# A hybrid decoder trunk on one core: the order of the high and low weight products within a unit of TensorE work

## The chip, the core and the metric

The kernel runs on one NeuronCore of one Trainium2 chip. The metric is the device time of one execution in microseconds (us), as the median of several executions. TensorE multiplies matrices, VectorE (DVE in the rows), ScalarE (ACT) and GpSimd (POOL) compute elementwise, and SyncE (SP) starts the DMA transfers.

## What is computed

A trunk of two layers is run for one prompt of 512 tokens and for 8 samples of 4 new tokens, with the same weights, all in 32-bit floats. Each layer is a half feed-forward block (SwiGLU), a mixer, and another half feed-forward block. The mixer of layer 0 is a convolution module, that of layer 1 gated linear attention (GLA).

```python
def swiglu_ffn(h, w_gate, w_up, w_down):
    return (jax.nn.silu(h @ w_gate) * (h @ w_up)) @ w_down

for i in range(DEPTH):
    x = x + 0.5 * swiglu_ffn(rms_norm(x, norm_ffn_pre[i]), ffn_w_gate[i, 0], ffn_w_up[i, 0], ffn_w_down[i, 0])
    h = rms_norm(x, norm_mix[i])
...
    x = x + y
    x = x + 0.5 * swiglu_ffn(rms_norm(x, norm_ffn_post[i]), ffn_w_gate[i, 1], ffn_w_up[i, 1], ffn_w_down[i, 1])
```

In the lines left out y is the mixer's result. The convolution module is a projection from 1024 to 2048 (`pw1`), a gate, a depthwise convolution of 31 taps, a layer norm and a projection (`pw2`). GLA projects to queries, keys, values, an output gate and a decay (`gz`, `gv`, `gr`, `gkq`), runs a recurrence over matrix states, and projects back (`gwo`). The model width is 1024 (8 blocks of 128), the feed-forward width 2816 (22 blocks). Outputs are the final normed activations and the new convolution and GLA states.

## The kernel before

The 544 tokens (512 and 32) stand along the free dimension, features along the 128 partitions. Every activation tensor is a row of blocks of 128 x 544.

**Three products for one.** A weight product in full precision is made of three products of a reduced 32-bit type. The weight `raw` is split into `w_hi` (a copy into the reduced type, by ScalarE, `high`) and `w_lo` (`raw - w_hi`, by VectorE, `low`); the activations likewise into `xg_hi` and `xg_lo`, or `h_hi` and `h_lo`. TensorE adds `w_hi * a_hi`, `w_hi * a_lo` and `w_lo * a_hi` in PSUM. Each product of a block is two matmuls, since 544 columns are two halves of 272 in two banks. Every matmul loads its 128 x 128 weights anew.

**Slots.** Weights come in slots of up to 8 blocks of 128 x 128, 512 KB each, numbered through the whole program (329 of them). SyncE loads a slot into one of 2 `raw` places, and waits before that for `w_split` of the slot that used the place. `w_hi` and `w_lo` are rings of 4 places. ScalarE writes `w_hi` of slot n after `w_done` of slot n - 4 and counts `w_high` up; VectorE waits for `w_high`, writes `w_lo` and counts `w_split` up. TensorE counts `w_done` up with the last matmul of a slot. Each engine's instructions stand in a fixed order, written out by hand, and semaphores join the engines.

**Units.** A unit is one output block of 128 x 544, in one of four pairs of PSUM banks. An up projection or a square one takes one slot for a unit (48 matmuls), a down projection three slots, of 8, 8 and 6 blocks (132 matmuls). VectorE takes the result out of PSUM and counts `evac` up; TensorE waits on `evac` before it writes over a pair.

**`slot_products`** makes the products of one slot. It waits for `w_split` of its slot, and then goes through the blocks k: for each of them six matmuls, `w_hi` with `a_hi`, `w_hi` with `a_lo`, `w_lo` with `a_hi`, two halves each. With `ready` it waits ahead of each block until the activation of that block is split: `x_split` for the first slot of the convolution's first projection (`pw1`) and for `gz`, the first slot of the GLA stage; `h_split` for the first unit of each down projection. With `halfway` a function is called ahead of the block in the middle: in the GLA output projection (`gwo`) it is `sample_kv(i)`, four matmuls for the samples' states `st`, which VectorE then updates (line 1903). **`wide_products`** (line 480 on) does the first two or four slots of the other stages at once and is a function of its own; the last unit of the program has its own code (line 1336).

**What follows the two slots that wait for `x_split`.** Behind the first slot of `pw1`, and behind `gz`, stands `pe_stat` (line 518): two matmuls that sum the squares of x, after `acc` of GpSimd (line 627). VectorE and ScalarE make the reciprocal root of it (lines 642 to 651, 661, 663), with which all evictions of that stage are scaled. `xg_hi` (line 602, ScalarE) and `xg_lo` (line 608, VectorE) of block m are made after x of block m has been updated with the result of the down projection (line 808, VectorE).

Of the kernel before, what the change touches and what calls it, by code (L numbers as in the profile page):

```python
# [42 lines left out]
def build(nc, x_prompt, x_sample, state_conv, state_gla, norm_ffn_pre, norm_mix, norm_ffn_post, norm_final,  # L43
# [7 lines left out]
    HALF = T // 2  # L51
# [18 lines left out]
    with ctx:  # L70
# [7 lines left out]
        def sb(name, shape, dt=F32):  # L78
            n = 4
            for d in shape[1:]:  # L80
                n *= d
            offset = taken[0]
            taken[0] += (n + 31) // 32 * 32
            return at(name, shape, dt, offset)
# [10 lines left out]
        w_hi = sb("w_hi", [P, RING, SLOT_K, P], F32R)  # L95
        w_lo = sb("w_lo", [P, RING, SLOT_K, P], F32R)
# [109 lines left out]
        ps = nc.alloc_psum_tensor("ps", [P, 8, 512], F32)  # L206
# [8 lines left out]
        def sem(name):  # L215
            return ctx.enter_context(nc.semaphore(name))
# [14 lines left out]
        w_high = sem("w_high")  # L231
        w_split = sem("w_split")
# [232 lines left out]

        def slot_products(pe, n, pair, a_hi, a_lo, nk=SLOT_K, k0=0, kt=SLOT_K, i=0, per=0, ready=None, halfway=None):

            pe.wait_ge(w_split, n + 1 + per * i)
            r = n % RING
            for k in range(nk):  # L470
                if ready is not None:
                    pe.wait_ge(ready[0], ready[1] + k + 1)
                if halfway is not None and k == nk // 2:
                    halfway()
                for w, a in ((w_hi, a_hi), (w_hi, a_lo), (w_lo, a_hi)):
                    for c in range(2):
                        last = nc.tensor.matmul(  # L477
                            ps[:, 2 * pair + c, 0:HALF], w[:, r, k, :], a[:, k0 + k, c * HALF:(c + 1) * HALF],
                            start=(k0 + k == 0 and w is w_hi and a is a_hi),
                            stop=(k0 + k == kt - 1 and w is w_lo))  # L480
            last.then_inc(w_done, 1)

        def wide_products(pe, n, pairs, a_hi, a_lo, ready, high_ready=None, between=None):
# [56 lines left out]
        def pe_ffn(pe, s):  # L540
            u0, s0 = s.up.u0, s.up.s0
            if s is f00:
                pe.wait_ge(evac, 2)
                pe.wait_ge(s_xo, 2)
                wide_products(pe, s0, [u0 % 4, (u0 + 1) % 4], xg_hi, xg_lo, (x_split, 0))

                pe.wait_ge(s_diag, TT + 1)
                bank = 2 * ((u0 + 3) % 4)
                for t in range(TT):
                    nc.tensor.matmul(ps[:, bank, t * P:(t + 1) * P], ones[:, :], rdiag[:, t, :], start=True, stop=True)  # L550
                nc.tensor.matmul(ps[:, bank + 1, 0:NS], ones[:, :], rdiag[:, TT, 0:NS], start=True, stop=True).then_inc(
                    s_stat, 1)
                slot_products(pe, s0 + 2, (u0 + 2) % 4, xg_hi, xg_lo)
                pe.wait_ge(s_r0, 1)
                slot_products(pe, s0 + 3, (u0 + 3) % 4, xg_hi, xg_lo)
            else:
                pe.wait_ge(evac, u0 - 2)
                wide_products(pe, s0, [u0 % 4, (u0 + 1) % 4], xg_hi, xg_lo, (x_split, M * s.q))
                pe.wait_ge(evac, u0)
                pe_stat(pe, s.e, (u0 + 3) % 4)  # L560
                slot_products(pe, s0 + 2, (u0 + 2) % 4, xg_hi, xg_lo)
                pe.wait_ge(s_nv, 3 * s.r + 1)
                slot_products(pe, s0 + 3, (u0 + 3) % 4, xg_hi, xg_lo)
# [1439 lines left out]
```

## Time and profile before

| | |
|---|---|
| median of 3 runs | 2128.21 us (2127.31 to 2129.12) |
| the profiled execution | 2128.8 us |
| its span, first to last instruction | 2127.1 us |
| TensorE matmul busy | 2086.6 us, 98% |
| VectorE busy | 990.8 us, 47% |
| ScalarE busy | 637.7 us, 30% |
| GpSimd busy | 142.7 us, 7% |
| DMA, mean share of 16 engines | about 31% |
| matmuls on line 477 | 3 x (3344 + 1524) |

All rows come from one profiled execution. Matmuls are pipelined: each row shows some 0.29 us for one, but they start closer together, so I read their pace from start to start. A share of busy time is a mean over stages; what an edit is worth has to be read at the place where it acts.

### The profile page before, as it was taken

Reading aid. Unit: us, or ns where it says so; the run is one execution under the profiler, and the core shown is the slowest. Engines: PE = TensorE matmul, PEld = TensorE weight load, DVE = VectorE, ACT = ScalarE, POOL = GpSimd, SP = SyncE. Lnnn points to the kernel's source line nnn. Section 1 sums busy time; section 2 is a strip of 40 time slices with the busy share of each in tenths; the row PEclk is TensorE's granted clock in tenths of the full one; section 3 lists DMA queues with packets and bytes.
Section 4 is the critical chain, followed back from the end, with each engine's and each line's share of the span. In section 5 each row is a group of like instructions: output and inputs, shape, how many; then the busy total and the mean of one; then the engine's idle time right before and its main releaser. Section 6 shows DMA issues by size and latency. Waiting matters only on the chain.

```text
span 2127.1 us, 39290 instructions
## 1 busy us (share of the span) xinstructions
PE 2086.6 (98%) x16373; PEld 2026.5 (95%) x16373; DVE 990.8 (47%) x1299; ACT 637.7 (30%) x899; POOL 142.7 (7%) x146
## 2 busy tenths in 40 slices
PE   8999999999899999999999999999999999999998
PEld 7999999987599999999999999999888899999998
DVE  4575433387655444433344443333455764444332
ACT  5222222222243222222322222222433532222222
POOL 2000001200021000011100000111000210000000
PEclk9999999999999999999999999999999999999999
DMA  5232323345323223232333332232224333332322
GB/s 165 80 92 85 89 82 92 94 119 141 85 60 99 82 86 88 87 90 82 88 90 89 89 89 82 84 91 82 73 61 130 104 116 89 89 88 83 95 83 70
DMA packets 351727, 194.83 MB, mean 92 GB/s; under 512 B 8636, under 2 KB 345758, under 8 KB 351628
## 3 DMA queue, kind: packets, MB, share of 16 engines
q1 hardware_dynamic: 345388, 185.10, 30.3%
q10 hardware_dynamic: 4560, 4.82, 0.7%
q0 software_dynamic: 1696, 3.73, 0.6%
q8 instruction: 62, 1.02, 0.2%
q14 instruction: 21, 0.17, 0.0%
HBM read 177.29 MB, written 8.05 MB: 87 GB/s over the span
## 4 chain that ended last, share of the span: by engine, by line
PE 92%; DVE 3%; ACT 2%; issue 1%; DMA 1%; SPq 1%; POOL 0%; DVEq 0%; ACTq 0%
PE ps L477 83%; PE ps L488 3%; PE ps L1067 1%; PE ps L1336 1%; ACT w_hi L455 1%; PE ps L1076 1%; SPq L886 0%; DMA raw<-in_ffn_w_gate 0%; DVE cv L1660 0%; DVE odd_sum L1660 0%; DMA raw<-in_conv_w_pw 0%; PE ps L1183 0%; DVE x L1721 0%; PE ps L1191 0%; DMA st<-in_state_gla 0%
## 5 line engine op out<-in xcount | busy, mean ns | idle before, releaser
L477 PE MATMUL ps<-xg_hi,w_hi 128*128 128x272 f32 x3344 | 696.8, 290 | 4.0 <-DVE tb L1677 2.0
L477 PE MATMUL ps<-xg_hi,w_lo 128*128 128x272 f32 x3344 | 693.8, 289 | 0.0
L477 PE MATMUL ps<-xg_lo,w_hi 128*128 128x272 f32 x3344 | 691.0, 288 | 0.0
L455 ACT ACTIVATE w_hi<-raw 128x1024 fp32r<-128x1024 f32 x329 | 348.2, 1059 | 1025.8 <-PE ps L477 977.7
L462 DVE TENSOR_TENSOR w_lo<-raw,w_hi 128x1024 fp32r<-128x1024 f32 x329 | 412.7, 1255 | 411.8 <-ACT w_hi L455 411.4
L477 PEld LDWEIGHTS ps<-xg_hi,w_hi 128*128 128x128 f32 x3344 | 527.4, 189 | 7.4 <-DVE tb L1677 3.1
L477 PEld LDWEIGHTS ps<-xg_lo,w_hi 128*128 128x128 f32 x3344 | 526.7, 189 | 0.0
L477 PEld LDWEIGHTS ps<-xg_hi,w_lo 128*128 128x128 f32 x3344 | 523.2, 189 | 0.0
L477 PE MATMUL ps<-h_hi,w_hi 128*128 128x272 f32 x1524 | 316.0, 289 | 1.4 <-DVE x L1721 0.9
L477 PE MATMUL ps<-h_hi,w_lo 128*128 128x272 f32 x1524 | 315.8, 289 | 0.0
L477 PE MATMUL ps<-h_lo,w_hi 128*128 128x272 f32 x1524 | 314.4, 288 | 0.0
L477 PEld LDWEIGHTS ps<-h_hi,w_hi 128*128 128x128 f32 x1524 | 239.6, 188 | 1.9 <-DVE x L1721 1.1
L477 PEld LDWEIGHTS ps<-h_lo,w_hi 128*128 128x128 f32 x1524 | 239.6, 189 | 0.0
L477 PEld LDWEIGHTS ps<-h_hi,w_lo 128*128 128x128 f32 x1524 | 237.9, 189 | 0.0
L778 DVE TENSOR_TENSOR tb<-ps,rB 128x544 f32<-128x544 f32 x88 | 63.7, 724 | 284.3 <-PE ps L477 284.3
L701 ACT ACTIVATE h_hi<-tb 128x544 f32 (+1 forms) x88 | 58.0, 659 | 178.1 <-DVE tb L783 178.1
L774 DVE TENSOR_TENSOR ta<-ps,rB 128x544 f32<-128x544 f32 x88 | 63.7, 724 | 98.4 <-PE ps L477 97.5
L785 DVE TENSOR_TENSOR h_lo<-tb,h_hi 128x544 f32 (+1 forms) x88 | 63.9, 726 | 82.6 <-ACT h_hi L701 82.6
L627 POOL TENSOR_TENSOR acc<-acc,sqt 128x544 f32<-128x544 f32 x35 | 64.7, 1849 | 2.8
L620 POOL TENSOR_TENSOR acc<-x 128x544 f32<-128x544 f32 x5 | 5.5, 1092 | 873.6 <-DVE x L808 817.9
L783 DVE TENSOR_TENSOR tb<-ta,tb 128x544 f32<-128x544 f32 x88 | 63.2, 719 | 0.0
L698 ACT ACTIVATE ta<-ta 128x544 f32<-128x544 f32 x88 | 56.8, 645 | 20.0 <-DVE ta L774 20.0
(273 smaller groups left out, 1213.2 us busy)
## 6 DMA issues: line engine op xcount, KB each, us to landing
raw<-in_ffn_w_gate SPq DMA_DIRECT2D x88, 512.0 KB, 3.8
raw<-in_ffn_w_up SPq DMA_DIRECT2D x88, 512.0 KB, 3.8
raw<-in_ffn_w_down SPq DMA_DIRECT2D x64, 512.0 KB, 4.0
raw<-in_gla_w_in SPq DMA_DIRECT2D x25, 512.0 KB, 3.8
raw<-in_ffn_w_down SPq DMA_DIRECT2D x32, 384.0 KB, 3.4
raw<-in_conv_w_pw SPq DMA_DIRECT2D x24, 512.0 KB, 4.4
u_shift<-uext SPq DMA_DIRECT2D x112, 66.0 KB, 2.0
raw<-in_gla_w_out SPq DMA_DIRECT2D x8, 512.0 KB, 4.2
```

Of the source, the lines that this page charges most:

```text
L455: nc.scalar.activation(w_hi[:, n % RING], raw[:, n % RAW], ACT.Copy).then_inc(w_high, 1)
L462: nc.vector.tensor_tensor(w_lo[:, n % RING], raw[:, n % RAW], w_hi[:, n % RING].bitcast(F32), ALU.subtract).then_inc(w_split, 1)
L477: last = nc.tensor.matmul(ps[:, 2 * pair + c, 0:HALF], w[:, r, k, :], a[:, k0 + k, c * HALF:(c + 1) * HALF], start=(k0 + k == 0 and w is w ...
L488: last = nc.tensor.matmul(ps[:, 2 * pairs[j] + c, 0:HALF], w[:, (n + j) % RING, k, :], a[:, k, c * HALF:(c + 1) * HALF], start=(k == 0 and ...
L627: last = nc.gpsimd.tensor_tensor(acc[:, :], acc[:, :], sqt[:, :], ALU.add)
L698: nc.scalar.activation(ta[:, p, :], ta[:, p, :], ACT.Silu).then_inc(a_done, 1)
L701: nc.scalar.activation(h_hi[:, 2 * i + p, :], tb[:, p, :], ACT.Copy).then_inc(h_high, 1)
L774: nc.vector.tensor_tensor(halves(ta[:, p, :]), bank_pair(pair), halves(rB[:, :]), ALU.mult).then_inc(evac, 1)
L778: nc.vector.tensor_tensor(halves(tb[:, p, :]), bank_pair((pair + 1) % 4), halves(rB[:, :]), ALU.mult).then_inc(evac, 1)
L783: nc.vector.tensor_tensor(tb[:, p, :], ta[:, p, :], tb[:, p, :], ALU.mult).then_inc(h_prod, 1)
L785: nc.vector.tensor_tensor(h_lo[:, 2 * i + p, :], tb[:, p, :], h_hi[:, 2 * i + p, :].bitcast(F32), ALU.subtract).then_inc(h_split, 1)
L1067: last = nc.tensor.matmul(ps[g * GROUP:(g + 1) * GROUP, 4 + m % 2, :], w_tap[:, m % 2, g, n, :], u_shift[m % 3][:, g, SHIFTS * n:SHIFTS * ...
```

## The change

Within `slot_products` the products with `w_hi` now run over all blocks of the slot first, and those with `w_lo` over all blocks afterwards. The wait for `w_split` at the head of the slot becomes a wait for `w_high`, and the wait for `w_split` stands between the two passes. The waits of `ready` and the call of `halfway` stay in the first pass. `w_done` is counted up by the last matmul of the second pass.

```diff
-            pe.wait_ge(w_split, n + 1 + per * i)
+            def products(k, w, a):
+                for c in range(2):
+                    last = nc.tensor.matmul(
+                        ps[:, 2 * pair + c, 0:HALF], w[:, r, k, :], a[:, k0 + k, c * HALF:(c + 1) * HALF],
+                        start=(k0 + k == 0 and w is w_hi and a is a_hi),
+                        stop=(k0 + k == kt - 1 and w is w_lo))
+                return last
+
+            pe.wait_ge(w_high, n + 1 + per * i)
             r = n % RING
             for k in range(nk):
                 if ready is not None:
                     pe.wait_ge(ready[0], ready[1] + k + 1)
                 if halfway is not None and k == nk // 2:
                     halfway()
-                for w, a in ((w_hi, a_hi), (w_hi, a_lo), (w_lo, a_hi)):
-                    for c in range(2):
-                        last = nc.tensor.matmul(
-                            ps[:, 2 * pair + c, 0:HALF], w[:, r, k, :], a[:, k0 + k, c * HALF:(c + 1) * HALF],
-                            start=(k0 + k == 0 and w is w_hi and a is a_hi),
-                            stop=(k0 + k == kt - 1 and w is w_lo))
+                products(k, w_hi, a_hi)
+                products(k, w_hi, a_lo)
+            pe.wait_ge(w_split, n + 1 + per * i)
+            for k in range(nk):
+                last = products(k, w_lo, a_hi)
             last.then_inc(w_done, 1)
```

The end of the first slot of `pw1` on TensorE, before; each row is a line, an instruction and what it waits for, and `acc` is the sum of squares:

```order
L477 MATMUL ps<-xg_hi,w_hi 128x272 [waits x_split]
L477 MATMUL ps<-xg_hi,w_hi 128x272
L477 MATMUL ps<-xg_lo,w_hi 128x272 x2
L477 MATMUL ps<-xg_hi,w_lo 128x272 x2
L518 MATMUL ps<-acc,ones 128x272 [waits s_acc]
L518 MATMUL ps<-acc,ones 128x272
L477 MATMUL ps<-xg_hi,w_hi 128x272 [waits w_split,evac]
```

And with the change (line numbers are 7 higher behind the helper, and its matmul is on line 470):

```order
L470 MATMUL ps<-xg_hi,w_hi 128x272 [waits x_split]
L470 MATMUL ps<-xg_hi,w_hi 128x272
L470 MATMUL ps<-xg_lo,w_hi 128x272 x2
L470 MATMUL ps<-xg_hi,w_lo 128x272 [waits w_split]
L470 MATMUL ps<-xg_hi,w_lo 128x272 x15
L525 MATMUL ps<-acc,ones 128x272 [waits s_acc]
L525 MATMUL ps<-acc,ones 128x272
L470 MATMUL ps<-xg_hi,w_hi 128x272 [waits w_high,evac]
```

The last wait for `x_split` stood ahead of the last 6 matmuls of the slot; now it stands ahead of the last 20, of which 16 take `w_lo`. `gz` is built in the same way.

The middle of the first slot of `gwo` that has a `halfway`, on TensorE, before; `kem` and `v_s` are the operands of `sample_kv`:

```order
L477 MATMUL ps<-h_lo,w_hi 128x272 x2
L477 MATMUL ps<-h_hi,w_lo 128x272 x2
L1282 MATMUL ps<-v_s,kem 128x256 [waits g_kem,g_vlo]
L1282 MATMUL ps<-v_s,kem 128x256 x3
L477 MATMUL ps<-h_hi,w_hi 128x272 x2
L477 MATMUL ps<-h_lo,w_hi 128x272 x2
L477 MATMUL ps<-h_hi,w_lo 128x272 x2
```

And with the change:

```order
L1289 MATMUL ps<-v_s,kem 128x256 [waits g_kem,g_vlo]
L1289 MATMUL ps<-v_s,kem 128x256 x3
L470 MATMUL ps<-h_hi,w_hi 128x272 x2
L470 MATMUL ps<-h_lo,w_hi 128x272 x2
L470 MATMUL ps<-h_hi,w_hi 128x272 x2
L470 MATMUL ps<-h_lo,w_hi 128x272 x2
L470 MATMUL ps<-h_hi,w_hi 128x272 x2
L470 MATMUL ps<-h_lo,w_hi 128x272 x2
L470 MATMUL ps<-h_hi,w_hi 128x272 x2
L470 MATMUL ps<-h_lo,w_hi 128x272 x2
L470 MATMUL ps<-h_hi,w_lo 128x272 [waits w_split]
L470 MATMUL ps<-h_hi,w_lo 128x272 x15
```

Ahead of `sample_kv` there were 24 matmuls of the slot and 24 behind it; now there are 16 ahead and 32 behind.

## Rows read from the trace of the kernel before

**Rows 1.** The page's busy time (share of the span) and instructions of each engine.
```profile
PE 2086.6 (98%) x16373; PEld 2026.5 (95%) x16373; DVE 990.8 (47%) x1299; ACT 637.7 (30%) x899; POOL 142.7 (7%) x146
```
**Rows 2.** The chain that ended last: start us, us, what, how many.
```profile
52.86 366.85 PE ps L477 x2928
...
1034.53 12.06 PE ps L488 x96
```
**Rows 3.** Waits: engine, line, waited for: us in total, times, longest us.
```profile
ACT w_hi L455 <- PE ps L477: 977.7, 279, 5.9
...
PE ps L1076 <- DVE cv L1670: 5.4, 1, 5.4
```
**Rows 4.** Timeline of `pw2`: start us, us, engine, line, operation, count, idle before.
```profile
609.59 1.23 DVE L462 TENSOR_TENSOR w_lo<-raw,w_hi 128x1024 fp32r<-128x1024 f32 x1 [12.12 <-ACT w_hi L455]
...
611.56 0.52 PE L477 MATMUL ps<-h_hi,w_hi 128*128 128x272 f32 x2 [0.85 <-DVE x L1721]
```
**Rows 5.** Stretches: us, busy us (count) by engine, PEclk, DMA share, GB/s.
```profile
660.00:780.00 120.00, 120.00 (x960) 120.00 (x959) 54.66 (x63) 34.89 (x42) 0.00 (x0) 1.00 0.32 92
820.00:1030.00 210.00, 210.00 (x1679) 210.00 (x1678) 76.66 (x81) 52.56 (x58) 18.57 (x13) 1.00 0.30 88
```
**Rows 6.** Timeline of the first slot of `pw1`.
```profile
419.53 0.41 PE L477 MATMUL ps<-xg_hi,w_hi 128*128 128x272 f32 x2
...
423.84 0.79 DVE L608 SCALAR_TENSOR_TENSOR xg_lo<-x,par,xg_hi  x1 [1.16 <-ACT xg_hi L602]
423.93 1.90 POOL L627 TENSOR_TENSOR acc<-acc,sqt 128x544 f32<-128x544 f32 x1
...
424.78 0.42 PE L477 MATMUL ps<-xg_hi,w_hi 128*128 128x272 f32 x2
...
425.88 1.19 PE L518 MATMUL ps<-acc,ones 128*128 128x272 f32 x4 [0.19 <-POOL acc L627]
```
**Rows 7.** Timeline of TensorE where it starts again in `pw1`.
```profile
463.83 0.52 PE L477 MATMUL ps<-xg_hi,w_hi 128*128 128x272 f32 x2 [1.25 <-DVE tb L1677]
464.19 0.29 PE L477 MATMUL ps<-xg_lo,w_hi 128*128 128x272 f32 x1
```
**Rows 8.** Timeline of `gz`.
```profile
1432.18 0.41 PE L477 MATMUL ps<-xg_hi,w_hi 128*128 128x272 f32 x2
...
1436.49 0.79 DVE L608 SCALAR_TENSOR_TENSOR xg_lo<-x,par,xg_hi  x1 [1.16 <-ACT xg_hi L602]
...
1438.64 1.16 PE L518 MATMUL ps<-acc,ones 128*128 128x272 f32 x4 [0.28 <-POOL acc L627]
```
**Rows 9.** Timeline of the start of the first down projection.
```profile
291.33 0.73 DVE L785 TENSOR_TENSOR h_lo<-tb,h_hi 128x544 f32 x1 [0.94 <-ACT h_hi L701]
...
299.26 0.41 PE L477 MATMUL ps<-h_hi,w_hi 128*128 128x272 f32 x2
```
**Rows 10.** Timeline of the end of `gwo`, VectorE and TensorE.
```profile
1700.33 0.63 PE L1282 MATMUL ps<-v_s,kem 128*128 128x256 f32 x4
...
1701.17 1.65 DVE L1903 SCALAR_TENSOR_TENSOR st<-st,dec,ps 128x256 f32<-128x256 f32 x4
1702.74 2.21 DVE L462 TENSOR_TENSOR w_lo<-raw,w_hi 128x1024 fp32r<-128x1024 f32 x1
1704.87 1.64 DVE L1903 SCALAR_TENSOR_TENSOR st<-st,dec,ps 128x256 f32<-128x256 f32 x4
...
1715.20 0.49 PE L488 MATMUL ps<-xg_hi,w_hi 128*128 128x272 f32 x2 [1.75 <-issue]
```
**Rows 11.** Stretches, columns as in rows 5; the last of line 477 alone.
```profile
460.00:468.00 8.00, 6.75 (x60) 4.69 (x50) 7.78 (x12) 3.97 (x5) 0.00 (x0) 1.00 0.58 152
561.50:564.90 3.40, 3.16 (x10) 2.35 (x11) 0.79 (x2) 0.00 (x0) 0.00 (x0) 0.51 0.91 245
...
1496.80:1507.00 10.20, 9.49 (x33) 7.99 (x33) 3.63 (x5) 6.74 (x6) 0.00 (x0) 0.50 0.11 30
...
1501.60:1507.00 5.40, 5.40 (x24) 5.40 (x25) 0.50 0.00 2
```

## The prediction

> **What bounds the kernel now.** I read the busy shares first, then the chain that ended last, then who waits for whom, and after that the timeline at the places where TensorE pauses. TensorE computes for 2086.6 us of a span of 2127.1 us [rows 1], and 83% of the chain that ended last is one line, the matmul of `slot_products`. In the middle of a feed-forward stage 2928 of these matmuls follow each other in 366.85 us [rows 2], which is 0.1253 us each; I call this the pace. A slot of 8 blocks has 48 matmuls and so takes 6.01 us. A change of order pays only where TensorE now waits for something that it could do without a little longer, and it costs where TensorE now just finds ready something that it will want earlier.
>
> The change drops the wait for `w_lo` at the head of a slot. Does anybody wait there today? In the list of waits the longest that ends on a matmul is 5.4 us, for a tensor of the convolution, and neither `w_lo` nor `w_hi` stands anywhere in it as the releaser of a matmul. It is the other way round: ScalarE waited 279 times, 977.7 us in all, for TensorE to give a place of the ring back before it could write `w_hi` [rows 3]. The weights run ahead. I looked for the slot where they run ahead least, and it is the fifth of the second projection of the convolution: its `w_lo` ends at 609.59 + 1.23 = 610.82 us, but TensorE starts that slot at 611.56 us, released by the eviction of a result [rows 4]. So the wait that is dropped ends last nowhere, and I put the gain at 0.
>
> **The change part by part.** *The same matmuls.* No matmul is added or removed. A slot has 32 products with `w_hi` and then 16 with `w_lo`. What a matmul costs in the new order the trace of before does not show. The nearest rows are those of `wide_products`, which has a third order (high, low, high in each block): 96 matmuls in 12.06 us [rows 2], 0.1256 us each, 0.0003 us above the pace, and those include some ten waits. The new order changes between `w_hi` blocks and `w_lo` blocks no more often than the old one, so I take 0. For the range I keep 0.0003 us either way; line 477 has 3 x (3344 + 1524) = 14,604 matmuls, which is 4.4 us up or down.
>
> *The added wait.* Each of the 312 slots that go through this helper (329, less 14 of `wide_products` and the 3 of the last unit) gets one more wait, in its middle. What an already fulfilled wait costs can be read by comparing stretches: in the up projection every 48 matmuls have two waits and a branch of the loop falls on every 192; in the down projection four waits fall on 132 matmuls. Both run at 960 matmuls in 120 us and 1679 in 210 us [rows 5], 0.125 us each to the last digit that these counts allow. I take 0 and leave the cost of up to 0.003 us per wait that the ten waits of [rows 2] would give (1 us in all) inside the 4.4 us above.
>
> *The wait for `x_split`, block by block: the term that counts.* Two slots read their activations while these are still being made: the first of `pw1`, at 419.53 us, and `gz`, at 1432.18 us. They wait for `xg_lo` of block k ahead of block k. The last block, k = 7, is late, because `x` of that block can only be updated when the last down projection is done: its `xg_lo` runs from 423.84 to 424.63 us [rows 6]. Before, block 7 is reached after 7 x 6 = 42 matmuls, at 419.53 + 42 x 0.1253 = 424.79 us, and the row of that matmul says 424.78 us: it just meets the data, 0.15 us behind. Now the high part reaches block 7 after 7 x 4 = 28 matmuls, at 419.53 + 3.51 = 423.04 us. TensorE must stand until 424.63 + 0.06 = 424.69 us (0.05 us lie between the end of `acc` at 423.93 + 1.90 = 425.83 us and the matmul that it releases at 425.88 us; I take 0.06), that is 1.65 us. After a stop the first pair takes 0.36 us in place of 0.25 us [rows 7], another 0.11 us. Left of the slot are 4 matmuls of the high part and 16 of the low part: 20 x 0.1253 = 2.51 us, so it has issued its last at 424.69 + 0.11 + 2.51 = 427.31 us.
>
> Not all of this reaches the end. Right behind the slot stands the matmul of the sum of squares (line 518), which waits for that `acc` of GpSimd and starts at 425.88 us, while the slot's own matmuls ended at 425.54 us. Now `acc` has been ready for long and the matmul starts at 427.31 us: **+1.43 us**. What is late next is everything: VectorE's reciprocal root, the evictions of the first two units, and the copies that SyncE issues for the convolution all hang on that matmul or on the end of this slot, so the whole stage moves by as much and I see nothing in it that takes it back.
>
> The same for `gz` [rows 8]: block 7 is wanted at 1432.18 + 3.51 = 1435.69 us, `xg_lo` ends at 1436.49 + 0.79 = 1437.28 us, TensorE goes on at 1437.34 us, and issues its last at 1437.34 + 0.11 + 2.51 = 1439.96 us. The sum of squares started at 1438.64 us before: **+1.32 us**.
>
> The Trainium skill has a rule on this, in "TensorE: Matmul & The Clock Gate", under "What happens when you issue a matmul": the engine may pull a weight load forward, but matmuls stay in program order. By it the 16 products with `w_lo` cannot pass the blocked block 7; were they free to, the stop would be filled and the sum would be 0.
>
> *The slots that wait for `h_split`* (the first three of each down projection) are not near it: in the first of these stages the last `h_lo` ends at 291.33 + 0.73 = 292.06 us, and the third slot, the one that reads it, starts at 299.26 us [rows 9]. *The slots cut in half by `sample_kv`*: its four matmuls stood after 24 matmuls of the slot and now stand after 16, 1.0 us earlier. VectorE's updates of `st` behind them stand in a fixed order with other work: the last group runs from 1704.87 us because `w_lo` ahead of it takes from 1702.74 to 1704.95 us [rows 10], not because of its matmuls, so nothing comes earlier. The last of them waits for an update that ends at 1701.17 + 1.65 = 1702.82 us and is now wanted at 1700.33 + 0.47 + 16 x 0.1253 = 1702.80 us: up to 0.2 us of stop, and it lies ahead of a pause of 1.75 us that ends at 1715.20 us [rows 10] and that no matmul of this helper sets. I count 0.
>
> **Sum**: 1.43 + 1.32 = 2.75 us. The profiled execution took 2128.8 us (a span of 2127.1 us and 1.7 us around it), 0.6 us over the median of 2128.21 us. So 2131.5 us against itself, and 2131.0 us as a median. That is 0.13%. A measurement of this kernel tells about 0.2%, 4.3 us, from no change, and this would be called the same.
>
> **The rivals.** *Nothing is lost* (2128.2 us): while block 7 is missing TensorE would go on with the 16 products of `w_lo`, 2.00 us of work, which fills a stop of 1.65 us. Against it: in the order of before, too, work that was ready stood behind waiting matmuls, as the whole slot behind the 5.4 us of [rows 3], and none of it went ahead.
>
> *Slower, by the clock.* The granted clock fell twice in the middle of the kernel, both times after TensorE had been idle: at 561.5 us, to 0.51 for 3.4 us, and at 1496.8 us, to 0.50 (1.2 GHz) until 1507.0 us [rows 11]. In the second fall 24 matmuls took 5.40 us, 0.225 us each. If each new stop let the clock fall as at 561.5 us, that would be 3.4 x (1 - 0.1253/0.225) = 1.5 us each and 3.0 us in all: 2134.0 us. It decides once a stop of 1.65 us in a dense stretch is enough for the clock to fall. Against it: ahead of 463.83 us TensorE was idle for 1.25 us [rows 7], and the clock stayed at 1.00 [rows 11].
>
> *Slower, by the pace or the waits*: at the upper bound of 4.4 us, 2131.0 + 4.4 = 2135.4 us. The same bound downwards gives 2126.6 us.
>
> *Slower, by issue.* If a weight load and a matmul took half the pace each merely to be issued, TensorE would be bound by its instruction stream, and each of the 312 added waits would cost 0.0626 us: 19.5 us, 2150.5 us. Against it: at that price two waits per 48 matmuls and four per 132 would differ by 0.0007 us a matmul and the loop's branches by more, and [rows 5] show one pace. The Trainium skill, in the same page under "Wait — 56ns, not 53.3ns?", says that with hardware decode off the sequencer spends about 62 ns on each matmul, which would be just this case.
>
> **How the numbers follow.** The two stops: 0.68. Nothing lost: 0.10. Clock: 0.06. Pace or waits upwards: 0.10; downwards: 0.04. Issue: 0.02. The predicted time is 2131.0 us. The runs of before spread by 0.9 us about their median. The range from 2127.8 to 2134.2 us takes in the two stops with the spread and a part of the bound of the pace, nothing lost, and the clock. Faster by over 0.2% (under 2124.0 us) takes the whole downward bound and no stops: 0.03. Slower (over 2132.5 us) is clock, pace upwards, issue, and a tail of 0.04 of the first case: 0.22. The same: 0.75.
>
> **What would show it.** In the timeline after: at about 424.7 and 1438.7 us (moved by the first stop) a `xg_hi,w_hi` matmul with some 1.5 us of idle time ahead, released by `xg_lo`; in the list of waits the pair matmul and `xg_lo` with two waits and about 3 us. The sum-of-squares matmul at 427.3 us, and at 1438.64 + 1.43 + 1.32 = 1441.4 us. The loops at 366.9 us per 2928 matmuls; another pace there is the rival of the pace. A granted clock below 1.00 at 425 or 1438 us is the rival of the clock. I am wrong in the large if order alone changes what a matmul costs.

## The result, and the profile after

The change takes **2135.89 us** (median of 7 runs, 2135.77 to 2137.71), the kernel before, run beside it, 2128.21 us (7 runs, 2126.60 to 2131.52). The ratio is 1.0036, with a 95% interval of 1.0025 to 1.0048: slower by 7.7 us. The forecast was 2131.0 us with a range up to 2134.2 us. The change came out 4.9 us above the forecast and 1.7 us above the range; the two stops on which the forecast rests are 2.75 us. One execution of e3_waits_only below took 8598.58 us and one of e4_third_order 6119.55 us, for a reason that no row shows, and their ratios leave these out.

The profiled execution after took 2135.8 us, with a span of 2134.1 us, 7.0 us more than before. Its busy time by engine, as in [rows 1]: TensorE is busy 7.5 us longer, with the same number of matmuls (its weight loads, PEld, 6.5 us longer); the other engines stay within 0.9 us.

```profile
PE 2094.1 (98%) x16373; PEld 2033.0 (95%) x16373; DVE 990.9 (46%) x1299; ACT 638.2 (30%) x899; POOL 143.6 (7%) x146
```

**The stops are there, and as long as forecast.** The timeline of TensorE after, in the first slot of `pw1` and in `gz` (start us, us, engine, line, operation, count, idle before and its releaser), which answers to [rows 6] and [rows 8]:

```profile
420.41 0.41 PE L470 MATMUL ps<-xg_hi,w_hi 128*128 128x272 f32 x2
...
423.68 0.41 PE L470 MATMUL ps<-xg_lo,w_hi 128*128 128x272 f32 x2
425.56 0.52 PE L470 MATMUL ps<-xg_hi,w_hi 128*128 128x272 f32 x2 [1.47 <-DVE xg_lo L615]
...
426.16 2.18 PE L470 MATMUL ps<-xg_hi,w_lo 128*128 128x272 f32 x16
428.18 1.08 PE L525 MATMUL ps<-acc,ones 128*128 128x272 f32 x4
...
1436.54 0.41 PE L470 MATMUL ps<-xg_hi,w_hi 128*128 128x272 f32 x2
...
1441.69 0.52 PE L470 MATMUL ps<-xg_hi,w_hi 128*128 128x272 f32 x2 [1.46 <-DVE xg_lo L615]
...
1444.31 1.08 PE L525 MATMUL ps<-acc,ones 128*128 128x272 f32 x4
```

TensorE issues 28 matmuls of the high part and stops until `xg_lo` of block 7 is there. The 16 matmuls with `w_lo`, whose data is ready, stand behind. From the first matmul of the slot to the sum of squares it was 425.88 - 419.53 = 6.35 us in `pw1` and is 428.18 - 420.41 = 7.77 us now: +1.42 us, against a forecast of +1.43. In `gz` it was 1438.64 - 1432.18 = 6.46 us and is 1444.31 - 1436.54 = 7.77 us: +1.31 us, against +1.32. The list of waits (engine, line, waited for: total us, times, longest) has the new pair:

```profile
PE ps L470 <- DVE xg_lo L615: 2.9, 2, 1.5
...
PE ps L470 <- ACT w_hi L455: 1.2, 1, 1.2
```

The second row is new in name only. Before, the same place (1553.56 us, now 1560.34 us) waited 1.17 us, put down to VectorE's `ta`; now it waits 1.17 us, put down to the `w_hi` for which the change has TensorE wait. The ScalarE wait of [rows 3] hardly moved, 980.5 us.

The clock stayed at 1.00 across both stops (stretches: us, busy us and count of PE, PEld, DVE, ACT, POOL, PEclk, DMA share, GB/s), also from 424.05 to 425.56 us and from 1440.20 to 1441.70 us, the stops themselves:

```profile
425.00:427.00 2.00, 1.44 (x11) 1.45 (x12) 0.50 (x1) 0.85 (x1) 2.00 (x2) 1.00 0.60 180
1441.00:1443.00 2.00, 1.31 (x10) 1.31 (x11) 0.64 (x1) 0.98 (x1) 2.00 (x2) 1.00 0.75 218
```

**The loops are slower, and that was not forecast.** The chain that ended last (start us, us, what, how many), after:

```profile
51.79 368.80 PE ps L470 x2928
...
652.34 385.70 PE ps L470 x3072
1038.04 12.05 PE ps L495 x96
1051.01 385.71 PE ps L470 x3072
...
1734.64 275.72 PE ps L470 x2196
```

The same four runs of matmuls in the kernel before; its 366.85 us for 2928 stand in [rows 2]:

```profile
649.68 384.85 PE ps L477 x3072
...
1047.50 384.86 PE ps L477 x3072
...
1728.41 275.11 PE ps L477 x2196
```

TensorE waits for nothing in these runs. The pace was 0.1253 us in all four (384.85 / 3072 = 0.12528). It is 368.80 / 2928 = 0.12596 us in the first stage and 385.70 / 3072 = 0.12556 us in the other three. `wide_products` (line 495), which the change does not touch, needs 12.05 us for 96, and 12.06 us before.

The two traces, place by place; each row but the last is the start of the same matmul, and the last column is what was added since the row above:

| place | before | after | after is later by | grown by |
|---|---|---|---|---|
| first loop begins | 52.86 | 51.79 | -1.07 | |
| first slot of `pw1` | 419.53 | 420.41 | 0.88 | 1.95 |
| sum of squares of `pw1` | 425.88 | 428.18 | 2.30 | 1.42, stop |
| second loop | 649.68 | 652.34 | 2.66 | 0.36 |
| third loop | 1047.50 | 1051.01 | 3.51 | 0.85 |
| first slot of `gz` | 1432.18 | 1436.54 | 4.36 | 0.85 |
| sum of squares of `gz` | 1438.64 | 1444.31 | 5.67 | 1.31, stop |
| fourth loop | 1728.41 | 1734.64 | 6.23 | 0.56 |
| end of the span | 2127.1 | 2134.1 | 7.0 | 0.77 |

The loads at the start happened to be 1.07 us quicker in the execution after. From there it lost 8.07 us: 2.73 us in the two stops and 5.34 us elsewhere. Of these, 4.26 us lie in the four loops (1.95, 0.85, 0.85 and 0.61 us), 11,268 of the 14,604 matmuls of `slot_products`. The last 1.08 us are a sum of gains and losses. The largest is a stretch of low clock in GLA, here in 18 us of each trace, before and then after:

```profile
1490.00:1508.00 18.00, 14.98 (x68) 12.36 (x67) 6.63 (x7) 11.89 (x13) 1.03 (x2) 0.72 0.18 50
```
```profile
1494.00:1512.00 18.00, 15.69 (x66) 12.28 (x65) 5.09 (x6) 9.57 (x12) 1.03 (x2) 0.67 0.26 73
```

The granted clock was near 0.50 (1.2 GHz) until 1507.0 us before and until about 1513.9 us after, and from the slots behind `gz` to the run of 384 matmuls behind them it took 62.81 us in place of 61.77 us. The experiments e1 to e4 below need 61.75 to 61.85 us for the same way, with either order, and e7, the change with one more matmul at the start, needs 62.81 us again. So the order alone does not bring this 1 us; what does is open. The loops are the larger part, and the experiments are about them.

### The profile page after: what moved, and what is told of

Its sections match the earlier page's. It is cut to its first block, busy times and chain, and to the rows that moved or that the text cites. A ratio compares the mean times of both kernels' runs of the same rounds, so it can differ in the third digit from the quotient of the medians.

```text
span 2134.1 us, 39290 instructions
## 1 busy us (share of the span) xinstructions
PE 2094.1 (98%) x16373; PEld 2033.0 (95%) x16373; DVE 990.9 (46%) x1299; ACT 638.2 (30%) x899; POOL 143.6 (7%) x146
## 4 chain that ended last, share of the span: by engine, by line
PE 93%; DVE 2%; ACT 1%; DMA 1%; issue 1%; SPq 1%; DVEq 0%; ACTq 0%
PE ps L470 85%; PE ps L495 3%; PE ps L1074 1%; PE ps L1343 1%; PE ps L1083 1%; SPq L893 0%; ACT w_hi L455 0%; DVE cv L1667 0%; PE ps L1164 0%; DMA pin<-in_gla_onorm_g 0%; DVE odd_sum L1667 0%; PE ps L1190 0%; PE ps L1198 0%; DMA st<-in_state_gla 0%; DMA raw<-in_conv_w_pw 0%
## 5 line engine op out<-in xcount | busy, mean ns | idle before, releaser
L455 ACT ACTIVATE w_hi<-raw 128x1024 fp32r<-128x1024 f32 x329 | 348.5, 1060 | 1028.9 <-PE ps L470 980.5
L470 PE MATMUL ps<-xg_hi,w_lo 128*128 128x272 f32 x3344 | 452.9, 288 | 0.0
L470 PEld LDWEIGHTS ps<-xg_hi,w_lo 128*128 128x128 f32 x3344 | 432.2, 188 | 0.0
L470 PE MATMUL ps<-h_hi,w_lo 128*128 128x272 f32 x1524 | 207.7, 288 | 0.0
L470 PEld LDWEIGHTS ps<-h_hi,w_lo 128*128 128x128 f32 x1524 | 197.5, 188 | 0.0
L631 POOL TENSOR_TENSOR sqt<-x 128x544 f32<-128x544 f32 x35 | 40.1, 1145 | 331.1 <-DVE x L815 290.2
```

The costliest lines, as they stand in the source:

```text
L455: nc.scalar.activation(w_hi[:, n % RING], raw[:, n % RAW], ACT.Copy).then_inc(w_high, 1)
L470: last = nc.tensor.matmul(ps[:, 2 * pair + c, 0:HALF], w[:, r, k, :], a[:, k0 + k, c * HALF:(c + 1) * HALF], start=(k0 + k == 0 and w is w ...
L631: nc.gpsimd.tensor_tensor(sqt[:, :], src[:, m, :], src[:, m, :], ALU.mult).then_inc(p_acc, 1)
```

## Experiments

"This" and "before" are medians from the same chip; a ratio has its 95% interval. The edits are shown against the change, those of e12 and e13 against the kernel before.

### Which part of the change costs what

**e1_no_stop** is the change, but the two slots that wait for `x_split` keep the order of before.

```diff
+            together = ready is not None and ready[0] is x_split
...
+                if together:
+                    last = products(k, w_lo, a_hi)
```

> The change, but the two slots that wait block by block for the split activations (first slot of pw1, and gz) keep the order of before. Theory (stops and pace are two separate costs): the two stops of 1.75 us in the timeline at 425.56 and 1441.69 us go, the loops keep the pace of the changed kernel (368.8 us for 2928 matmuls in the first stage, 385.7 us for 3072 in the later ones), and the median falls by 2.7 us, from 2135.9 to 2133.2. Rival (the stops are all that matters and the pace is an accident of that execution): the median comes down to about 2128 to 2129.

**e2_order_only** has the new order with one wait for `w_split` at the head, as before.

```diff
-            pe.wait_ge(w_high, n + 1 + per * i)
+            pe.wait_ge(w_split, n + 1 + per * i)
...
-            pe.wait_ge(w_split, n + 1 + per * i)
```

> The new order of products, but one wait for w_split at the head of the slot as before, none in the middle. Theory A (the order itself costs the pace, some 0.0003 us a matmul): the loops stay at 385.7 us for 3072 matmuls and the median at 2135 to 2137. Rival B (the wait in the middle of the slot costs some 0.014 us each, 48 x 0.0003): the loops return to 384.9 us, only the stops are left, and the median is about 2131.

**e3_waits_only** has the old order with the two waits of the change.

```diff
-            pe.wait_ge(w_split, n + 1 + per * i)
-            for k in range(nk):
+                if k == 0:
+                    pe.wait_ge(w_split, n + 1 + per * i)
                 last = products(k, w_lo, a_hi)
```

> The order of products of before, but the two waits of the change: w_high at the head of the slot, w_split ahead of the first product with w_lo, after four matmuls. Theory A (order costs): loops at 366.9 us for 2928 and 384.9 us for 3072 matmuls, median 2128 to 2129. Rival B (the added wait costs): loops at 368 us or more and 385.7 us, median 2132 to 2134.

**e4_third_order** puts the order of `wide_products` (high, low, high in each block) into `slot_products`.

```diff
-            pe.wait_ge(w_high, n + 1 + per * i)
+            pe.wait_ge(w_split, n + 1 + per * i)
...
                 products(k, w_hi, a_hi)
-                products(k, w_hi, a_lo)
-            pe.wait_ge(w_split, n + 1 + per * i)
-            for k in range(nk):
-                last = products(k, w_lo, a_hi)
+                products(k, w_lo, a_hi)
+                last = products(k, w_hi, a_lo)
```

> One wait at the head, and in every block high with a_hi, low with a_hi, high with a_lo: the order of the helper that takes several slots at once, whose 96 matmuls took 12.06 us before (0.1256 us each). No stop, since the data of a block are wanted when before. Theory A (the order sets the pace, and this one has the pace of those 96): loops of 3072 matmuls at 385.8 us, median about 2133. Rival B (the 0.1256 us there come from that helper's ten waits): loops at 384.9 us, median 2128 to 2129.

| kernel | this, us | ratio to before (2127.75 us) | first loop, 2928 | third loop, 3072 |
|---|---|---|---|---|
| e1_no_stop | 2132.45 | 1.0021 (1.0012 to 1.0030) | 368.80 | 385.71 |
| e2_order_only | 2136.06 | 1.0039 (1.0026 to 1.0052) | 368.80 | 385.71 |
| e3_waits_only | 2127.13 | 0.9995 (0.9986 to 1.0005) | 366.84 | 384.86 |
| e4_third_order | 2127.51 | 0.9997 (0.9988 to 1.0006) | 366.84 | 384.86 |

The first loop in the chains of e2, then e3, then e4, from which the table is read:

```profile
51.68 368.80 PE ps L470 x2928
```
```profile
52.24 366.84 PE ps L470 x2928
```
```profile
52.81 366.84 PE ps L470 x2928
```

The order alone is the whole effect (e2), and the waits alone are nothing (e3). Without the stops the change is still slower by 0.21%, 4.7 us between the medians, with exactly the loops of the change (e1); the stops are the 3.6 us between e1 and e2, where the trace of the change has 2.73 us of them; the 0.9 us between are not explained. (Its two idle times are 1.47 and 1.46 us; the 1.75 us of the expectation are in no row.) And e4 takes away the row on which I sized the term: `wide_products` runs at 0.1256 us a matmul, yet with the order of its blocks `slot_products` runs at 0.1253. What sets `wide_products` apart is then something else. It has some ten waits in 96 matmuls, which would be 3 ns for each, while the 312 waits added in e3 cost nothing that shows; and it goes through two slots side by side, with other weights and other banks in turn, which e4 does not do. Neither was tried by itself.

### Does the rule lie in how often the weights change between high and low?

**e5_three_passes** makes three passes over the slot: high with `a_hi`, high with `a_lo`, low with `a_hi` (the `x_split` slots as in e1).

```diff
-                products(k, w_hi, a_lo)
...
+                for k in range(nk):
+                    products(k, w_hi, a_lo)
+                pe.wait_ge(w_split, n + 1 + per * i)
+                for k in range(nk):
+                    last = products(k, w_lo, a_hi)
```

> Three passes over the blocks of a slot instead of two: high with a_hi, then high with a_lo, then low with a_hi; the two slots that wait for the split activations keep the order of before, so there is no stop. Theory C (in the later stages of the changed kernel the pass with w_lo, which reads one activation tensor alone, runs at 0.1250 us a matmul and the pass with w_hi, which changes between a_hi and a_lo, at 0.1258; a pass on one tensor is the fast one): loops at 384.0 us for 3072 matmuls, median 2124 to 2126. Rival D (long passes are slow whatever they read): loops at 385.7 us or more, median 2132 or more.

It took 2125.85 us against 2127.59 us, a ratio of 0.9992 (0.9983 to 1.0001): the same. Its executions lie between 2123.64 and 2129.62 us, those of before between 2125.76 and 2128.99 us, and the profiled one is the slowest. Its chain is what counts:

```profile
51.81 368.46 PE ps L470 x2928
...
650.16 386.56 PE ps L470 x3072
...
1049.70 384.01 PE ps L470 x3072
```

The second and the third loop are the same instructions, and one runs at 0.1258 us, the other at 0.1250; the fourth, 274.50 us for 2196, is at 0.1250 too. So each of my two expectations came true in two loops of the four. One order has two paces, on either side of the pace of before, and holds each through a whole loop. Where pauses of 0.5 us stand between groups of 132 matmuls, in the last down projection, the groups take 16.51 and 16.61 us by turns, which are the same two paces.

**e6_two_blocks** alternates after two blocks, not eight. **e7_one_filler** and **e8_two_fillers** are the change with one and two more warming matmuls ahead of the first loop, 2 and 4 in the trace's count of instructions, for the guess that the pace follows the place of the loop in the count of matmuls. The edit of e7:

```diff
-            filler_products(0, xin[:, 0, 0:SEQ], 3)
+            filler_products(0, xin[:, 0, 0:SEQ], 4)
```

> Passes over two blocks only: eight matmuls with w_hi, four with w_lo, then the next two blocks. Theory D (the cost grows with the length of a pass): loops between 384.9 and 385.7 us for 3072 matmuls. Theory E (the cost comes from a pattern of four matmuls that falls into step with something of a period of eight; a pattern of six or twelve does not fall into step): the pace of before, 384.9 us, in all stages.

> The changed kernel with one more filler matmul on ones ahead of the first stage (4 in place of 3), nothing else. Theory E (falling into step: the pace of a stage hangs on how many matmuls stand ahead of it): the stages change their pace, the first one from 368.8 us for 2928 matmuls, or the later ones from 385.7 us for 3072. Rival F (the pace belongs to the order and the stage): 368.8 and 385.7 us again.

> The changed kernel with two more filler matmuls ahead of the first stage (5 in place of 3). Theory E: another pace than 368.8 us for 2928 or 385.7 us for 3072 in some stage, and another than with one filler. Rival F: 368.8 and 385.7 us again.

One execution each took 2137.78, 2138.27 and 2137.37 us. The loops of e7 and e8 are those of the change to 0.01 us (368.79 and 368.80 us; 385.70 to 385.71 us), so the guess falls for shifts by 2 and 4; an odd one was not tried. e6 is slower than the change in the later stages, 0.1261 us, outside both of my expectations, and faster in the first, 373.89 us for 2976, which is 0.1256 us:

```profile
652.37 387.40 PE ps L470 x3072
```

So the number of changes between high and low does not order the paces. A slot of 48 matmuls has 16 of them in the order of before and in e4 (0.1253 us both), 8 in e6 (0.1256 and 0.1261 us), and 2 in the change (0.1256 and 0.1260 us) and in e5 (0.1250 and 0.1258 us).

### TensorE alone

**e9_streams** leaves out all of the computation. TensorE runs bare streams of 288 matmuls, in the order of before, of the change, of e5, of e6 and in five others, without a wait inside a stream. Every other engine is idle meanwhile, and from 50 us on, 6 us into the first stream, so are the transfers.

> A kernel that leaves out all of the computation and measures TensorE by itself: streams of 288 matmuls (6 slots of 48) on tiles at the same places as in the kernel, in the order of before, of the change, in three passes, in passes over two blocks, and in simpler ones (pairs of a_hi and a_lo only; one tensor only; one weight tile only; one half only; the halves apart), each several times, behind pauses of about a microsecond that differ by 30 to 120 ns. No other engine works. Theory G (the pace is a property of TensorE's own stream, with two values for some orders, chosen by how a stream begins): before always 0.12528 us, the change 0.12556 or 0.12597, three passes 0.1250 or 0.1258, in some streams the one and in others the other. Rival H (the slower values come from the other engines' access to the same memories): one value for each order, 0.1250 to 0.1253.

Rows of its chain: line 46 is the order of before, 54 of the change, 62 three passes, 70 two blocks, 94 the same weights and activations over and over.

```profile
44.12 36.35 PE ps L46 x288
...
154.76 36.55 PE ps L54 x288
...
191.81 36.28 PE ps L62 x288
...
265.68 36.52 PE ps L62 x288
...
376.64 36.44 PE ps L54 x288
...
524.36 36.59 PE ps L70 x288
...
857.55 36.75 PE ps L94 x288
```

A row holds 0.28 us beyond count times pace (the first pair behind a pause is slower, and the last matmul runs out), so the paces are (36.35 - 0.28) / 288 = 0.1252 for the order of before, 0.1259 and 0.1256 for the change, 0.1250 and 0.1258 for three passes, 0.1261 for two blocks. These are the values of the kernels to 0.0001 us, both of them for the change and for three passes; of the two of e6 the 0.1256 did not come up in three streams. So neither waits nor other engines nor transfers are needed for these paces: **the order of the matmuls sets them, with TensorE alone at work**. Which of its two values an order takes it does not settle: of the five streams in three passes one took 0.1258, of the five in the order of the change one took 0.1256.

**e10_places** also leaves out the computation and repeats one matmul 144 times, moving one thing at a time: the column at which the activations begin, the weights, the bank, the number of columns.

> Bare streams again, all of the computation left out: 144 times the same matmul, each stream twice behind different pauses. Varied one at a time: the place from which the moving columns are read (shifts of 4 to 128 columns, 16 to 512 bytes), the weight block, the tensor, the number of columns (240 to 288), and alternation between two banks, two halves or two weight blocks. In the streams before, one half alone ran at 0.1233 us and one weight tile with alternating halves at 0.1267 us. Theory I (a matmul's time hangs on where in memory its columns start, as against the weights that are loaded meanwhile): the shifts give different paces between 0.120 and 0.130 us, with a pattern in steps of 16 columns or more; alternation of banks alone changes nothing. Rival J (it hangs on the bank of the result or on a change of operand): all shifts give one pace, and two_banks or two_weights another.

The chain; lines 45, 52, 80 are start columns 0, 4 and 48 with 272 columns; lines 157, 164, 171, 178, 185 have 240, 256, 264, 280 and 288 columns from column 0.

```profile
43.09 18.52 PE ps L45 x144
...
62.14 18.32 PE ps L45 x144
80.96 18.20 PE ps L52 x144
...
232.29 18.04 PE ps L80 x144
...
646.81 16.41 PE ps L157 x144
...
680.67 17.55 PE ps L164 x144
...
716.79 17.56 PE ps L171 x144
...
752.95 18.68 PE ps L178 x144
...
791.34 19.25 PE ps L185 x144
```

272 columns cost 0.1267 or 0.1253 us from column 0 (the same instructions, two values again), 0.1244 from column 4, 0.1233 from column 48. 64 columns further on the values are the same again: 80, 96 and 112 cost as 16, 32 and 48 (0.1267, 0.1267 and 0.1233 us). The weights and the bank gave no value of their own. The cost of more columns from column 0 is uneven: 256 and 264 columns both take 0.1200 us, 280 take 0.1278. The Trainium skill, in "TensorE: Matmul & The Clock Gate" under "Wait — 56ns, not 53.3ns?", gives N / 2.4 GHz and about 2.5 ns from start to start for N columns. For 272 columns that would be 115.8 ns, an estimate from that figure. These streams, which load weights for each matmul in the reduced type, are 8 to 11 ns above it at 272 columns and not on a line; here the measurement decides.

### From the steps to a version

If the cost of columns is uneven, then two halves of 272 need not be the cheapest way through 544. **e11_splits** runs bare streams in the order of before with other splits.

> Bare streams, the computation left out: 192 matmuls in the order of before with the 544 columns split not in 272 and 272 but in s and 544 - s, s from 224 to 288; the order of the change at s = 256 and 264; and single matmuls of 248 to 280 columns from column 0 and from column 8. Theory I (a matmul's time goes in steps with its number of columns and the place where they start): 240, 256, 264, 272, 280 and 288 columns took 0.1120, 0.1200, 0.1200, 0.1253 to 0.1267, 0.1278 and 0.1316 us from column 0, so s = 264 gives (0.1200 + 0.1278) / 2 = 0.1239 us a matmul and s = 272 the known 0.1253. Rival K (time only follows the number of columns and evens out): 0.1253 us for every s.

The chain; line 73 is 256 and 288 columns, 87 is 264 and 280, 101 the split of before, 115 is 288 and 256.

```profile
244.61 24.23 PE ps L73 x192
...
344.26 24.39 PE ps L87 x192
...
443.87 24.34 PE ps L101 x192
...
543.97 24.10 PE ps L115 x192
```

Less 0.28 us and by 192: 0.1247, 0.1256, 0.1253 and 0.1241 us. The single durations don't add up: 264 columns at 0.1200 and 280 at 0.1278 would have a mean of 0.1239, and the pair runs at 0.1256. Neighbours matter, or the start column: the second part of a pair does not begin at column 0, and from column 8 single matmuls of 264 columns take 0.1222 us in this run. Either way a split has to be run.

**e12_split_264** and **e13_split_288** are the kernel before, complete, with 264 and 280, and with 288 and 256 columns in place of 272 and 272. The first part now ends at the end of its bank and the second begins at the start of the next, so that VectorE still takes out one piece; in the bare streams both parts begin at the start of a bank.

```diff
+    SPLIT = 288
...
+        def out_part(pair, c):
+            return ps[:, 2 * pair + c, 512 - SPLIT:512] if c == 0 else ps[:, 2 * pair + c, 0:T - SPLIT]
...
-                            ps[:, 2 * pair + c, 0:HALF], w[:, r, k, :], a[:, k0 + k, c * HALF:(c + 1) * HALF],
+                            out_part(pair, c), w[:, r, k, :], a[:, k0 + k, part(c)],
```

> The kernel before, in its own order, but each block's two matmuls take 264 and 280 columns in place of 272 and 272, the first at the end of its bank and the second at the start of the next, so that evictions still read one piece. Theory I: 0.1239 us a matmul in place of 0.1253; with some 15,900 such matmuls the median falls by 15,900 x 0.0014 = 22 us, to about 2106. Rival K: no change, 2128.

> The kernel before, in its own order, with 288 and 256 columns in place of 272 and 272. In the bare streams this split ran at 0.1239 us a matmul, 272 and 272 at 0.1253, and 264 and 280 at 0.12555, which is to 0.00001 us what the whole kernel then showed. Theory I (bare streams give the kernel's pace, whatever the kernel does beside): loops at 0.1239 us, 380.6 us for 3072 matmuls, and the median falls by 15,900 x 0.0014 = 22 us to about 2105. Rival K: no change, 2127 to 2128.

e12, for which I had expected 2106 us from the single durations: 2133.34 us against 2127.19 us, ratio 1.0027 (1.0017 to 1.0036). e13: **2109.36 us** (2106.75 to 2110.44) against 2128.31 us, ratio **0.9912 (0.9898 to 0.9925)**. The third loop of e12, and two of e13:

```profile
1049.42 385.73 PE ps L485 x3072
```
```profile
51.94 362.82 PE ps L485 x2928
...
644.09 380.64 PE ps L485 x3072
```

Both run at the pace of their bare stream, 0.1256 us, and 0.1239 us against 0.1241 us in e11 and 0.1239 us in the best stream of e14. The results stand elsewhere in the banks there, so it is the split of the columns that sets the pace. e13 beats the kernel before by 0.9% and the change by 1.2%: 0.0014 us on each of 14,604 matmuls is 20 us, and 19.0 us were measured.

**e14_more_splits** leaves out the computation once more and tries splits around 288, and other orders at 288.

> Bare streams, the computation left out: 192 matmuls, each stream three times, for splits of 284 to 320 columns in the order of before, and for the third order, the order of the change and three passes at 256 and at 288. Theory I: with 288 and 256 columns all places at which the columns start are multiples of 32 (128 bytes), and the orders differ no more, or less than at 272: 0.1239 us each. Rival L (order matters as much as at 272): the change 0.0003 us or more above before at 288 too.

Rows of its chain: lines 52, 94, 108 and 122 have 288 and 256 columns in the order of before, of `wide_products`, of the change, and in three passes.

```profile
117.46 24.07 PE ps L52 x192
...
567.33 24.08 PE ps L94 x192
...
715.52 24.37 PE ps L108 x192
...
865.14 24.44 PE ps L122 x192
```

288 is the best of the splits tried (284 gave 0.1250 to 0.1256 us, 292 and more 0.1255 us and up). I had expected the orders to differ no more at 288. They differ more than at 272: 0.1239 us for the first two, 0.1255 for the change, 0.1258 for three passes. In this stream the order of the change gives back all of the gain over 0.1253 us. With the parts the other way round, 256 and 288 columns, the order of before and that of the change cost the same, 0.1247 us (24.23 us for 192 both, in e11 and e14). What an order costs hangs on the split.

## Why the prediction was wrong, step by step

- **"So I take 0" for the same matmuls: the step that failed.** It measured 0.0003 us a matmul in three of the loops and 0.0007 us in the first, 4.3 us in the four loops together and 4.7 us for the whole kernel without the stops (e1), where I had put 0 with a bound of 4.4 us either way. The bound was used up. Two pieces of the reasoning were wrong. The excess of `wide_products` was taken for a sample of another order, and e4 shows that the order within its blocks costs nothing. And the argument that the new order changes between high and low no more often counted something that does not settle the pace: 16 changes a slot run at 0.1253 us, 8 slower than 2 in the later stages, and e5 with as few as the change has a pace on either side. That the bound had the right size was luck.
- **The two stops: right**, 1.42 and 1.31 us against 1.43 and 1.32 us, and TensorE went on at 5.15 us from the start of each slot, as worked out (5.16 us). TensorE did not go on with the `w_lo` products, so *nothing is lost* fell. By the rule of the Trainium skill that the prediction names ("TensorE: Matmul & The Clock Gate", "What happens when you issue a matmul") matmuls stay in program order, and the trace agrees: 16 ready ones stood behind idle times of 1.47 and 1.46 us.
- **Gain 0 from the dropped wait: right.** The slot with the least lead starts as before on the eviction and not on the weights. The timeline after, which answers to [rows 4]:

```profile
612.25 1.23 DVE L462 TENSOR_TENSOR w_lo<-raw,w_hi 128x1024 fp32r<-128x1024 f32 x1 [12.12 <-ACT w_hi L455]
...
614.23 0.52 PE L470 MATMUL ps<-h_hi,w_hi 128*128 128x272 f32 x2 [0.85 <-DVE x L1728]
```

- **Added wait 0: right** (e3: 366.84 against 366.85 us), and with it the rival by issue, 19.5 us, fell.
- **`sample_kv` and `h_split` 0: right.** No matmul waits for `h_lo` in the list after. The stop of up to 0.2 us in front of a pause is there: the last call of `sample_kv` and its four matmuls take 0.2 us longer than the calls before (line 1289, at 1709.58 us), and the pause behind, 1.75 us before, is 1.11 us. From the sum of squares of `gz` to the fourth loop 0.56 us were added. That is a balance: some 1,400 matmuls of `slot_products` at 0.0003 to 0.0007 us, which are 0.4 to 1.0 us, and 1 us more on the way with the low clock, less the shorter pause and a shorter wait for a transfer.
- **The clock**: 1.00 at both stops, so that rival fell. In the place where it had fallen before, it stayed low for longer in this execution, about 1 us that no part of the prediction had; e1 to e4 do not show it.
- **The sum**: 2.75 us of stops came to 2.73; with the pace at its upper bound the rival *slower, by the pace or the waits* gave 2135.4 us, and 2135.89 us were measured. It was the case that came true, by the pace and not by the waits, and I gave it 0.10. With 14,604 such matmuls a term whose sign was unknown and whose bound was 60% larger than the forecast itself should have had a larger share, and the range should have reached its end.

**What stays open.** Why the order sets the pace, and what chooses between two paces of one order. Two or four more matmuls ahead do not (e7, e8), and it needs no other engine (e9). The values depend on where the columns begin and how many there are (e10, e11). My guess is that it lies in how TensorE reads the activations or writes the results; no run tells which, and the profile has no row for it.

## What to carry to other kernels

When nearly the whole time is one matmul shape, its order, its start column and its split are sizes to be measured. A bare stream of 192 or 288 of them on an otherwise idle core gave the pace of the full kernel to 0.0002 us, here for 0.3% lost and 0.9% won; where an order had two paces, the stream did not tell which one a stage would take, and with e6 it missed one of them. A pass over all blocks must not wait for the last block while ready work stands behind it in program order: a wait that is just met after 42 matmuls is missed after 28, and the loss could be worked out to 0.01 us from a few rows. And a row that is slower by 0.0003 us is evidence on the order only when the order is all in which it differs.

## What the hardware showed that I had not expected

- The same instructions have two stable paces: 384.01 and 386.56 us for the same 3072 matmuls in one execution (e5), 18.52 and 18.32 us for 144 repeats of one matmul (e10).
- The pace depends on the column at which the activations begin: 0.1253 or 0.1267 us at 0, 0.1244 at 4, 0.1233 at 48, for 272 columns.
- Columns are not paid one by one: from column 0, 8 more are free from 256 to 264, and 16 more from there cost 0.0078 us. From column 8, 264 columns take 0.1222 us.
- The cost of an order hangs on the split: the order of the change costs 0.0016 us a matmul at 288 and 256 columns, 0.0003 or 0.0007 us at 272 twice, and nothing at 256 and 288.
- 288 and 256 columns are cheaper than 272 twice, 0.1239 against 0.1253 us a matmul in the kernel.
